# The recurrence of an RWKV-7 mixer on one core: T turned for two heads at a time, GpSimd's input work one step ahead, TensorE's steps written out

## The reference, cut to what matters

```python
def rwkv7_scan(r, w, k, v, a, b):
    """S[v_idx,k_idx]: S <- S diag(w) + (S a) b^T + v k^T; y = S r."""
    ...
kk = k * k_k;  kk = kk * rsqrt(max(sum(kk * kk), 1e-24))
k = k * (1.0 + (a - 1.0) * k_a)
y = rwkv7_scan(r, decay, k, v, -kk, kk * a)
y = group_norm(y) * gn_w + gn_b
bonus = sum(r * k * r_k) * v
return (y + bonus) * g
```

## Time and profile before

| | us |
|---|---|
| median of 3 runs | 3570.32 (3564.42 to 3578.72) |
| the profiled execution's own time | 3570.77 |
| its span (first to last instruction) | 3568.9 |
| stretch of the recurrence (steps 0 to 16) | about 1298 to 2003 |
| busy in the span: PE / DVE / ACT / POOL | 3111.6 / 2019.4 / 1596.5 / 879.0 |

### The profile page before, as it was taken

How to read it: one execution, slowest core, us unless ns; L and a number is a source line. 1 busy time by engine, 2 the same in 40 slices (tenths; PEclk the granted TensorE clock), 3 DMA queues, 4 the chain that set the end, 5 groups by cost and what they waited for, 6 DMA issues and landing times. The chain is left out here.

```text
span 3568.9 us, 76160 instructions
## 1 busy us (share of the span) xinstructions
PE 3111.6 (87%) x27464; PEld 2515.2 (70%) x27464; DVE 2019.4 (57%) x2950; ACT 1596.5 (45%) x2656; POOL 879.0 (25%) x1064
## 2 busy tenths in 40 slices
PE   7999999988898848888888599569899999996899
PEld 5776878865666637777778488457777777774687
DVE  4333761017777724444444233668788788885555
ACT  3332211007777723333333111057777777775332
POOL 1001320002141366766674100000000000000343
PEclk9999999999999969999999799679999999998899
DMA  5444357444000031211110466536877866773343
GB/s 166 171 171 156 127 179 251 142 132 107 7 16 7 12 125 44 80 63 62 62 62 15 138 215 214 200 110 244 316 284 262 338 258 248 294 264 138 127 147 118
DMA packets 230272, 541.77 MB, mean 152 GB/s; under 512 B 26208, under 2 KB 62176, under 8 KB 221824
## 3 DMA queue, kind: packets, MB, share of 16 engines
q1 hardware_dynamic: 211696, 471.48, 37.5%
q0 software_dynamic: 11552, 41.95, 3.2%
q10 hardware_dynamic: 6768, 24.64, 1.7%
HBM read 408.52 MB, written 129.51 MB: 151 GB/s over the span
## 5 line engine op out<-in xcount | busy, mean ns | idle before, releaser
L559 PE MATMUL p_z<-w_in_part,hn_split 128*128 128x512 f32 x2304 | 538.7, 394 | 8.7 <-DVE w_in_part L388 4.5
L559 PEld LDWEIGHTS p_z<-w_in_part,hn_split 128*128 128x128 f32 x2304 | 435.3, 190 | 100.1 <-DMA hn_split<-s_hT 5.0
L1670 DVE TENSOR_TENSOR e_w_part<-w_gate_up_sb,e_w_part 128x1024 fp32r<-128x1024 f32 x380 | 441.1, 1220 | 105.2 <-ACT e_w_part L1665 105.2
L1665 ACT CAST e_w_part<-w_gate_up_sb 128x1024 fp32r x380 | 372.3, 1046 | 134.0 <-PE pe_y L2420 71.0
L2408 PE MATMUL pe_gate<-e_w_part,e_xT 128*128 128x512 f32 x1128 | 288.6, 414 | 32.8 <-DVE e_w_part L1670 32.8
L2408 PE MATMUL pe_up<-e_w_part,e_xT 128*128 128x512 f32 x1128 | 274.8, 399 | 16.7 <-DVE e_w_part L1670 16.6
L2420 PE MATMUL pe_y<-e_w_part,e_hT 128*128 128x512 f32 x1128 | 277.2, 402 | 7.3 <-DVE e_w_part L1670 7.3
L2408 PEld LDWEIGHTS pe_gate<-e_w_part,e_xT 128*128 128x128 f32 x1128 | 219.1, 198 | 84.7 <-DVE e_w_part L1670 24.4
L2408 PEld LDWEIGHTS pe_up<-e_w_part,e_xT 128*128 128x128 f32 x1128 | 208.8, 188 | 81.2 <-DVE e_w_part L1670 33.1
L2420 PEld LDWEIGHTS pe_y<-e_w_part,e_hT 128*128 128x128 f32 x1128 | 210.4, 190 | 55.1 <-DVE e_w_part L1670 7.7
L1670 DVE TENSOR_TENSOR e_w_part<-w_down_sb,e_w_part 128x1024 fp32r<-128x1024 f32 x188 | 223.5, 1222 | 21.7 <-ACT e_w_part L1665 19.1
(11 more groups left out here) (422 smaller groups left out, 5946.9 us busy)
## 6 DMA issues: line engine op xcount, KB each, us to landing
w_gate_up_sb<-in_w_gate_dram SPq DMA_DIRECT2D x32, 2048.0 KB, 15.1
w_gate_up_sb<-in_w_up_dram SPq DMA_DIRECT2D x32, 2048.0 KB, 19.8
w_down_sb<-in_w_down_dram SPq DMA_DIRECT2D x32, 2048.0 KB, 9.8
hn_split<-s_hT SPq DMA_DIRECT2D x48, 1024.0 KB, 5.1
s_y<-e_y ACTq DMA_DIRECT2D x47, 512.0 KB, 7.2
s_hT<-hn_split SPq DMA_DIRECT2D x16, 1024.0 KB, 6.5
s_y<-d_zeros SPq DMA_DIRECT2D x16, 1024.0 KB, 6.6
s_zr<-z_stage SPq DMA_DIRECT2D x48, 256.0 KB, 2.0
```

The lines of the kernel that those rows point to most:

```text
L559: last = nc.tensor.matmul(bank, hs[m % 3][:, a, k, :].bitcast(F32R), w_part(c, b)[:, k, :].bitcast(F32R), start=(k == 0 and a == b == 0), ...
L1665: return nc.scalar.copy(high, src)
L1670: return nc.vector.tensor_tensor(low, src, high, ALU.subtract)
```

## The change

1. `Tr0` to `Tr4` become one job each for all heads: four 128x128 transposes, each of two heads and both chunks, instead of sixteen 64x64 matmuls. The result lies with the head in the partition's upper or lower half, so it has its own tile `TP`; `X` now splits by chunk ("a" is chunk 0, all heads) and also has the head in the partition. Each half of `TX` needs both halves of `X`, and each `X` needs both halves of the level before. `TX5` is split in two like the others. The bank of a job is looked up by `bank_of` and its last owner by `before_in_bank`, since the number of main jobs is no longer a multiple of 6.
2. GpSimd's input chain (`ahead`) for tile i+2 runs in step i, behind `Kh`, `Rh`, the bonus product `rk` and `T_init`, and ahead of the tail's `rsy`. It has a semaphore of its own (`AHEAD`). It is left out in the last steps, and runs twice before step 0 (for tiles 0 and 1).
3. TensorE's order of fillers is another one, and its 14 steps are written out instead of looped. The lists of ScalarE and VectorE follow: `G2` and `TX2` now stand behind `ssk`, `MN` behind `TX2`, `TX4` ahead of the mean of `y`, `TX5` behind `s2`.

```diff
+AHEAD_EV = ["rkv", "kk0"]
-POOL_EV = ["rkv", "kk0", "rsk", "ex", "b", "Kh", "Rh", "rk", "T_init", "rsy", "bv", "out"]
+POOL_EV = ["rsk", "ex", "b", "Kh", "Rh", "rk", "T_init", "rsy", "bv", "out"]
...
+            def ahead(i, s, j):
+                pool.wait_ge(z_in[s], ((i + 2) // 2 if isinstance(i, int) else j + 2 - s) * 64 + 64)
+                pool.tensor_tensor(rkv[s][:], rkv[s][:], z[s][:], ALU.subtract)
+                pool.drain()
+                pool.tensor_tensor(rkv[s][:], rkv[s][:], mu[:], ALU.mult)
+                pool.drain()
+                AHEAD.in_order("rkv")
+                pool.tensor_tensor(rkv[s][:], rkv[s][:], z[s][:], ALU.add).then_inc(AHEAD.sem, 1)
+                pool.drain()
+                AHEAD.in_order("kk0")
+                pool.tensor_tensor(kk0[:], rkv[s][:, RW:2 * RW], k_k[:], ALU.mult).then_inc(AHEAD.sem, 1)
...
                 ev("T_init", lambda: pool.tensor_copy(T[n][:], i64[:].unsqueeze(1).broadcast_to([P, HV, CK])))
+                if not isinstance(i, int) or i < TILES - 2:
+                    ahead(i, s, j)
                 if "tail" in what:
                     pool.wait_ge(DV.sem, DV.value("s2", i))
...
-                def tr(level, f):
-                    chunked(f"Tr{level}{f}", hs_of(f), lambda b, h, r: nc.tensor.matmul(cols(b, h // 2, CK), T[s][r, h, :], i64[r, :], start=True, stop=True),
-                            (DV, ("G3" if level == 0 else f"TX{level}") + f, 0))
+                def tr(level):
+                    def make(b):
+                        for p in range(4):
+                            last = nc.tensor.transpose(b[:, p * P:(p + 1) * P], T[s][:, 2 * p:2 * p + 2, :].rearrange("p h n -> p (h n)"), ident[:])
+                        return last
+                    job(f"Tr{level}", make, (DV, "G3b" if level == 0 else f"TX{level}b", 0))
...
-            steps(pe, step)
+                level(1); w_("a"); filled(1); w_("b")
+                level(2); g12("G2", 3); filled(2); two_jobs(("MN0", "MN1"), mn, (AC, "Wb", 0))
+                level(3); two_jobs(("RT0", "RT1"), rt); filled(3); each("Y0", range(HV), y0); s_(0)
+                level(4); s_(1); two_jobs(("Ya", "Yb"), y_, (DV, "RT1", 0), (DV, "S0", 0)); filled(4)
+                chunked("D", range(HV), d_, (DV, "G2b", 0), (AC, "vcopy", 1)); job("pc", chunk_ends)
+                level(5); t_(0); t_(1); filled(5); t_(2); t_(3)
...
+            for i in range(1, TILES - 1):
+                step(i, i % 2, {"main", "tail", "prep"}, None)
```

More of the change, by code:

```diff
@@ L1005 @@
 AB = "ab"
-PE_JOBS = (["cum", "G3a", "G3b", "G1a", "G1b", "Tr0a", "Tr0b", "Wa", "X1a", "X1b", "Wb", "TX1a", "TX1b", "G2a", "G2b",
[3 rows of a table removed]
+PE_JOBS = ["cum", "G3a", "G3b", "G1a", "G1b",
[5 rows of a table added]
 PREP_JOBS = ("cum", "pc", "T0", "T1", "T2", "T3")
 TAIL = ("Wa", "Wb", "MN0", "MN1", "RT0", "RT1", "Y0", "S0", "S1", "Ya", "Yb", "sqy", "s1", "yc", "s2", "yn", "ysum", "rsy", "out")
[L1012 to L1016, removed]
-POOL_EV = ["rkv", "kk0", "rsk", "ex", "b", "Kh", "Rh", "rk", "T_init", "rsy", "bv", "out"]
+PREP = PREP_JOBS + ("P", "cumsb", "Pex", "sqk", "vcopy", "kp", "ssk", "kkn", "Ah", "Bh", "bon", "T_init", "rsk", "ex", "b", "Kh", "Rh", "rk", "bv")
+ACT_EV = ["P", "cumsb", "Tr0", "X1a", "X1b", "Wa", "sqk", "Wb", "Tr1", "X2a", "X2b", "Pex", "Tr2", "X3a", "X3b", "Y0",
+          "Tr3", "X4a", "X4b", "D", "sqy", "pc", "vcopy", "Tr4", "X5a", "X5b", "T0", "T1", "T2", "T3", "Tr5"]
+DVE_EV = ["G3a", "G3b", "G1a", "G1b", "TX1a", "TX1b", "kp", "ssk", "G2a", "G2b", "TX2a", "TX2b", "MN0", "MN1", "kkn", "RT0", "RT1", "TX3a", "TX3b",
+          "S0", "S1", "Ya", "Yb", "TX4a", "TX4b", "s1", "yc", "Ah", "Bh", "s2", "TX5a", "TX5b", "bon", "yn"]
+AHEAD_EV = ["rkv", "kk0"]
+POOL_EV = ["rsk", "ex", "b", "Kh", "Rh", "rk", "T_init", "rsy", "bv", "out"]
 MAIN_JOBS = [n for n in PE_JOBS if n not in PREP_JOBS]
@@ L1020, with bank_of, before_in_bank @@
 CHUNKS = (slice(0, CK), slice(CK, 2 * CK))
+def bank_of(name):
+    return MAIN_JOBS.index(name) % BANKS if name in MAIN_JOBS else BANKS + PREP_JOBS.index(name) % 2
+def before_in_bank(name):
+    k = PE_JOBS.index(name)
+    for back, names in ((0, PE_JOBS[:k]), (1, PE_JOBS[k:])):
+        same = [other for other in names if bank_of(other) == bank_of(name)]
+        if same:
+            return same[-1], back
 def phase_rwkv(nc, t, ident):
@@ L1234, in step @@
                 ev("out", mul(yo[:], yo[:], g[n][:]))
-            steps(pool, step)
+            ahead(-2, 0, None)
+            step(-1, 1, {"prep"}, None)
+            step(0, 0, {"main", "prep"}, None)
+            with pool.Fori(0, (TILES - 2) // 2 - 1) as j:
+                step(j * 2 + 1, 1, {"main", "tail", "prep"}, j)
+                step(j * 2 + 2, 0, {"main", "tail", "prep"}, j)
+            step(TILES - 3, 1, {"main", "tail", "prep"}, None)
+            step(TILES - 2, 0, {"main", "tail", "prep"}, None)
+            step(TILES - 1, 1, {"main", "tail"}, None)
+            step(TILES, 0, {"tail"}, None)
         @block.scalar
@@ L1454, in ready @@
                     for name in names:
-                        ring, size = (MAIN_JOBS, BANKS) if name in MAIN_JOBS else (PREP_JOBS, 2)
-                        k = ring.index(name)
-                        e, other = owner(ring[k - size])
-                        if k >= size or not first:
-                            asked.append((e, other, 0 if k >= size else 1))
+                        last, back = before_in_bank(name)
+                        if not (back and first):
+                            asked.append((*owner(last), back))
                     for e in (AC, DV, PO):
```

113 lines of the change are left out of this document (49 added, 64 removed), and 8 rows, old and new, of the table PE_JOBS.

## The result

| | before | after |
|---|---|---|
| median, 12 runs each | 3570.01 us (3560.0 to 3578.72) | 3586.91 us (3579.76 to 3599.55) |
| profiled execution | 3570.77 us | 3591.94 us |
| its span | 3568.9 us | 3590.1 us |
| mean granted clock | 0.943 | 0.923 |

The ratio is 1.0052 (95%: 1.0039 to 1.0065). The forecast was 3548 us, 22 us faster. The time lies in the stated range, at its slow end, and the kernel became 17 us slower.

The account below looks back on a forecast made before the run. No engine was full: the step is a chain through several of them. 13 x (42.0 - 42.5) = -6.5 us, with the edges -23, against 3570.77 gave 3548 us; range 3492 to 3588.

Parts of the forecast that it names:

- Turns behind the input chain: VectorE's `yc`, `Ah` and `Bh` each wait for a whole GpSimd chain operation; `Bh` ends at +36.1, before +29.7.
- rival of short collisions: GpSimd gives way to VectorE or they hardly meet; GpSimd's round sets a step of 37.2 us: 3485 us, chance 0.13.
- TensorE fetches the same kind of straight code inside a turn now, so I add no new fetch cost: In TensorE's written-out steps, instruction fetch was given no added cost.
- `kkn` at +16.5: VectorE's `kkn` starts at +15.9, takes 0.7 instead of 1.75 us, and so ends at +16.5 in the step.
- third rival: TensorE's straight code has fetch holes too, giving back up to 2.7 us a step: 3565 us, chance 0.15.
- From `T0` to the next `cum`: End of TensorE's step: transposes and `TX5` work, plus 1.5 us for lower clock; next `cum` at +40.5 before the clock loss.
- slower rival: After the gap before `T0`, half clock lasts some 10 us into the next step: 45.5 us a step, 3593 us, chance 0.17.
- The step: Each of the 13 whole steps was to take 42.0 us against 42.5.
- Edges: Outside the 13 whole steps: step 14 -8, step 15 -4.5, step 0 -4 us, together -16.5.
- The written-out program: TensorE's loop turn of 3.34 us and about half the half-clock time behind it go: 2.7 us per step gross.
- Joint `Tr`: Joint transposes save 1.0 us of TensorE per step, but halves wait for each other; taken as 0, between -1 and +1.
- Signs: Expected in the trace after, among others: PE idle 7 to 9 us ahead of `T0`, `Pex` no longer a long wait.

Follow-up runs that it names:

- e6_split: The kernel after, with subtract, multiply and add of GpSimd's input chain each cut into three operations of 128x512: 3532.89 us.
- e1_loop: The kernel after, with TensorE's steps 1 to 14 as a loop of seven turns again: 3631.78 us.
- e2_unroll: The kernel before, with only TensorE's steps written out instead of looped: 3538.77 us.
- e10_joint: The kernel before's job order and input chain at the step's end, with joint transposes and TensorE's steps written out: 3551.73 us.
- e12_move: e10_joint with GpSimd's whole input chain moved behind `T_init`: 3604.32 us.
- e5_small: The kernel after, with the loads inside the loop cut to 16 columns of each tensor: 3564.55 us.

## Why the prediction was wrong, step by step

*Turns behind the input chain: right.* From the end of `kkn` to that of `Bh` the forecast had 36.1 - 16.5 = 19.6 us; measured 39.06 - 19.45 = 19.61. That the two agree to 0.01 is luck: the chain starts 0.6 us earlier behind `kkn` than forecast in the step shown, the first turn is taken by the scaling and not by `yc`, and single steps take 19.1 to 20.5 us. e6_split bears out the mechanism: shorter turns, and 54 us less. The rival of short collisions is out. The Trainium skill, "SBUF — State Buffer", "Who interferes with whom", with its lock for a whole instruction, is in agreement at 3.44 us too: `Ah` and `Bh` took 3.92 and 3.90.

*"TensorE fetches the same kind of straight code inside a turn now, so I add no new fetch cost": this step failed*, and with it `kkn` at +16.5: it ends at +19.45, 2.95 us later. The holes in and ahead of `MN` take 3.16 us a step. Before, they took 1.13, of which 0.3 are "issue". What I missed is what lies beside the code: the burst of loads now meets `MN`, and `kkn` stands behind `MN` in VectorE's list. The prediction had the cause in its hands: it says that the loads are sent behind `bv` and only asks whether they come in time, not that `bv` moves with the chain and what they then run beside. With small loads `kkn` ends at +16.97, 0.47 from the forecast. The third rival had such holes, but took them for a price of the written-out program, half hidden in the gap before `T0`. e1_loop has them without that program, and nothing hides them: `b`, `T_init`, the chain and `Bh` hang on `kkn`, so that the gap moves with it.

The Trainium skill, "Runtime: NRT & Kernel Launch", "Instruction fetch mechanics", says that instructions come in blocks of 16 KiB over a DMA queue and that crossing a block is mostly hidden. The packets of 16 KB in the trace agree with the first half; the second does not hold behind a burst of loads.

*From `T0` to the next `cum`.* I had 4.25 + 1.5 for the lower clock; measured 45.42 - 39.16 = 6.26, so 0.5 more. The half clock lasts 14.7 us a step and not 4 to 5, but 5.2 of them lie inside the gap itself, where TensorE has nothing to do, 5.0 between `T0` and the next `cum`, and 4.4 between +8 and the gap. In the first 8 us of a step there is none. So the slower rival, half clock through the next step's `G3`, `G1` and first levels, is out: it gives 3593 us, close to the measured time, by a cause that carries 0.5 of the 3.5 us that it asked for.

*The step.* 42.0 + 2.95 + 0.5 = 45.45, measured 45.42.

*Edges: right in sum, by luck.* 21.2 (the difference of the spans) - 13 x 2.90 = -16.5, as forecast. By place: -4.5 in step 0 and the preparation (forecast -4), -8.9 in step 14, which from its `G3` to the next one now needs 32.7 us (-8), but -0.1 behind it (-4.5). The 4.4 missing there are made up by 1.4 more than forecast in the first two, and by -2.9 ahead of the recurrence's first `cum`, where the forecast had nothing and the code is the same.

*The written-out program: the total right, its step not.* -2.7 a step in the forecast, 35 us; e2_unroll gives -31 in all, but -1.31 a step. Before, the six steps with a turn took 44.4 us and the others 40.9, so the turns were worth at most 1.65 a step: the half clock behind them, priced at 1 us a step, cost next to nothing. And the new holes beside the loads are in e2_unroll already. e1_loop gives +45 with the rest.

*Joint `Tr` at 0, within 1 us a step.* +0.33 a step, inside the bound; 3552 against 3539 us in all. Whether the halves that wait for each other or the new banks cost it stays open.

*Signs.* `Pex` was to be no long wait any more; it waits 3.0 us a step, 4.6 before. The gap ahead of `T0` was to be almost 9 us and is 6.8, since the holes had already made TensorE late.

By parts then: written out -31, joint transposes +13, chain moved +53 (e10_joint to e12_move), new order -17 (e12_move to after), together +17 before rounding. The last two are 35 together, where the forecast's other terms left about +12. Such differences depend on the order in which the parts are added; what holds for the whole is the step: by this sum, without the 13 x 2.95 = 38 us of the failed term the change would have been faster, near 3549 us. e5_small takes back 2.48 of the 2.95; the rest of the term was not taken away in any run.

*How far the cause is shown.* That the loads make most of the holes is shown by e5_small. That it is the fetch of instructions that waits behind them is read from the traces: the packets that don't start beside the loads, and the 13 idle stretches that all end 1.2 to 1.5 us behind one. The 1.11 us that stay with small loads are the same kind of hole beside no loads; why they come is open.

## What to carry to other kernels

Before an operation is moved on GpSimd, list what VectorE does beside the new place with two inputs in SBUF: each such instruction waited for a whole one of GpSimd here, so cut GpSimd's long operations into pieces before moving anything. Then list which loads wait for an operation behind the moved one: they move with it. For a hole of "issue" in straight code look at the DMA view and its instruction packets first; ask where a burst of loads will lie after the change, and what stands behind it. A column that reads 0 may only mean that the wait stands one job earlier. A change of several parts is priced part by part: here one part alone gained 32 us, and the sum lost 17.

## What the runs showed of the hardware

- Instruction packets (16 KB) didn't start for 11 us beside 2 MB of loads at up to 408 GB/s, and TensorE stood still for up to 5.0 us in the kernel after; it went on 1.2 to 1.5 us behind the end of the next packet. The turn of the loop had cost 3.34 us each two steps.
- An operation of GpSimd over 128x1536 (3.44 us alone) holds a VectorE operation with two inputs in SBUF for 3.9 us. It holds a small scaling with one input too (128x8, 0.17 us alone): 1.12 us at 1583.48, up to 3.44 us in e1_loop, and in each of these cases the scaling ended 0.03 us behind GpSimd's operation.
- With a gap of 7 us in each step the lower clock lasted 14.7 of 45.4 us, 5.2 of them inside the gap; with one of 3.3 us in each second step it was 4.05 of 42.5. In the kernel after it was over before each next `cum`.
